# First norm computed with tokens on rows, c spread by a transfer, scale weights loaded ahead of shift weights; last norm applied while the output is turned back

## What is computed

```python
c_act = jax.nn.silu(c)                                  # c: 1024 values, one c per block
mod = (c_act @ w_ada[l] + b_ada[l]).reshape(B, N_SUB, 3, D_MODEL)   # shift, scale, gate of each step

def norm_mod(h, j):
    shift = mod[:, j, 0][:, None, :]
    scale = mod[:, j, 1][:, None, :]
    return _rms(h) * g_norm[l, j] * (1.0 + scale) + shift           # _rms: h / sqrt(mean(h*h) + eps)
...
x = x + gt2 * f                                         # the tenth step's residual
return rmsnorm(x, g_final)                              # the last norm, no shift
```

## Time and profile before

| | us |
|---|---|
| median of three timed runs | 1726.49 (1723.31 to 1727.04) |
| profiled execution | 1721.48 |
| its span, first to last instruction | 1719.6 |
| TensorE busy | 1644.6 |
| VectorE busy | 1324.5 |
| ScalarE busy | 905.6 |
| GpSimd busy | 96.8 |

### The profile page before, as it was taken

One profiled execution on the slowest core, in us unless ns is written; L12 is line 12 of the kernel. 1 busy time (PEld: TensorE's weight loads), 2 busy tenths in 40 slices (PEclk: granted clock), 3 DMA queues, 4 the chain that ended last, 5 costly groups with the idle time before them and its releaser, 6 DMA issues.

```text
span 1719.6 us, 31950 instructions
## 1 busy us (share of the span) xinstructions
PE 1644.6 (96%) x13282; PEld 1611.2 (94%) x13282; DVE 1324.5 (77%) x2089; ACT 905.6 (53%) x1554; POOL 96.8 (6%) x136
## 2 busy tenths in 40 slices
PE   2999999999999999999999999979999998899998
PEld 2999998999999999998999999968999998799998
DVE  7788889688888888888688888947888888385553
ACT  3444457664454544467554545645545456464443
POOL 6000000010000000100120001001000000010000
PEclk6999999999999999999999999989999999999999
DMA  8688675347877787854377878412787862145551
GB/s 327 244 326 318 270 282 196 123 175 310 320 289 278 284 324 295 316 205 168 113 273 299 323 286 308 144 52 99 289 324 304 308 249 103 70 146 198 176 192 50
DMA packets 56881, 402.19 MB, mean 234 GB/s; under 512 B 6574, under 2 KB 6706, under 8 KB 8992
## 3 DMA queue, kind: packets, MB, share of 16 engines
q1 hardware_dynamic: 55136, 394.97, 61.1%
q0 software_dynamic: 1600, 5.18, 1.0%
HBM read 399.06 MB, written 1.05 MB: 233 GB/s over the span
## 4 chain that ended last, share of the span: by engine, by line
PE 82%; DVE 12%; ACT 4%; issue 2%; DMA 0%; DVEq 0%; ACTq 0%
PE PS L494 81%; DVE WL L1559 3%; DVE ring L1584 2%; DVE SCR L1562 2%; DVE SCR L1559 1%; ACT SCR L1405 1%; ACT WH L1126 1%; DVE HL L1562 1%; DVE X L1562 1%; DVE SCR L1556 1%; ACT HH L1159 0%; DVE SMALL L1934 0%; DVE SQ L1562 0%; DVE SCR L1896 0%; DVE SMALL L1895 0%
## 5 line engine op out<-in xcount | busy, mean ns | idle before, releaser
L1559 DVE TENSOR_TENSOR WL<-ring,WH 128x1024 fp32r<-128x1024 f32 (+1 forms) x508 | 600.4, 1216 | 190.5 <-ACT WH L1126 190.2
L494 PE MATMUL PS<-HH,WH 128*128 128x256 f32 (+1 forms) x2640 | 651.9, 286 | 21.2 <-ACT WH L1126 18.5
L494 PE MATMUL PS<-HL,WH 128*128 128x256 f32 (+1 forms) x2640 | 640.5, 283 | 0.0
L1126 ACT ACTIVATE WH<-ring 128x1024 fp32r<-128x1024 f32 (+1 forms) x508 | 511.5, 1049 | 98.5 <-PE PS L494 53.5
L494 PEld LDWEIGHTS PS<-HH,WH 128*128 128x128 f32 x2640 | 497.7, 190 | 27.7 <-ACT WH L1126 19.2
L494 PEld LDWEIGHTS PS<-HL,WH 128*128 128x128 f32 x2640 | 495.6, 190 | 0.7
L494 PE MATMUL PS<-HH,WL 128*128 128x256 f32 (+1 forms) x2640 | 375.8, 280 | 2.0 <-DVE WL L1559 1.8
L494 PEld LDWEIGHTS PS<-HH,WL 128*128 128x128 f32 x2640 | 339.4, 189 | 3.3 <-DVE WL L1559 3.3
L1584 DVE CUSTOM_DVE_ANT_0 ring<-ring,CB,VC 128x1024 f32<-128x1024 f32 x240 | 317.5, 1347 | 0.0
L494 PE MATMUL PS<-AH,WL 128*128 128x256 f32 x1056 | 298.8, 283 | 0.0
L494 PE MATMUL PS<-AL,WH 128*128 128x256 f32 x1056 | 298.8, 283 | 0.0
(11 more groups left out here) (194 smaller groups left out, 1491.1 us busy)
## 6 DMA issues: line engine op xcount, KB each, us to landing
ring<-in_up SPq DMA_DIRECT2D x88, 1024.0 KB, 5.7
ring<-in_ada SPq DMA_DIRECT2D x72, 1024.0 KB, 6.9
ring<-in_ffn SPq DMA_DIRECT2D x66, 1024.0 KB, 4.8
ring<-in_mod SPq DMA_DIRECT2D x48, 1024.0 KB, 7.1
ring<-in_down SPq DMA_DIRECT2D x44, 1024.0 KB, 6.1
ring<-in_win SPq DMA_DIRECT2D x32, 1024.0 KB, 6.8
ring<-in_wout SPq DMA_DIRECT2D x16, 1024.0 KB, 4.8
ring<-in_winv SPq DMA_DIRECT2D x4, 1024.0 KB, 5.0
```

The lines of the kernel that those rows point to most:

```text
L494: return e.matmul(out, lhsT, rhs, start=start, stop=stop, skip_group_check=skip)
L1126: e.activation(half_of(i)[0], slot_of(("unit", u))[:, w * (i % 2):w * (i % 2) + w], ACT.Copy).then_inc(s_hi, 1)
L1559: return e.tensor_tensor(out, a, b, op)
```

## The change

- **Loads.** c of both blocks comes as two rows (`crow`); `spread_c` is now a transfer that writes one row to all 128 partitions of CB. That of the first block is issued third, that of the second behind load 13. x is issued behind the third ada panel. The scale panels 4 to 7 are loaded ahead of the shift panels 0 to 3.
- **Silu** is applied by ScalarE on CB, 128x1024, at once (first block at the start, second in the first feed-forward's step 16).
- **First norm.** ScalarE squares x_rows with a running sum per row (a token), makes the root per token and scales x_rows into xr_rows by it. TensorE turns both x_rows (for X) and xr_rows. ScalarE then makes SQ and HH of each chunk straight from PSUM, with gain and shift. VectorE does panels 4 to 7, `gains`, then one half of panels 0 to 3 and one chunk's remainder in turn. GpSimd's first additions are gone.
- **Last norm.** The gain is multiplied into X chunk by chunk (XG, ScalarE; the last on VectorE). TensorE turns XG back two chunks behind, between the matmuls of `out_proj`, and sums the squares per token with one-column matmuls. The root per token is applied by the copies from PSUM to OUT, half on ScalarE, half on VectorE.

```diff
-        loads = [("ada", i) for i in range(FIRST_ADA)] + [("unit", 0)]
+        loads = [("ada", (i + 4) % 8) for i in range(FIRST_ADA)] + [("unit", 0)]
...
@@ sync
-            e.dma_start(x_rows, A["x"].rearrange("(t p) d -> p t d", p=128)).then_inc(s_xload, 16)
+            def spread_c(v):
+                row = bass.AP(tensor=crow.tensor, offset=crow.offset + D * v, ap=[[0, 128], [1, D]])
+                e.dma_start(CB[:, v, :], row).then_inc(s_cload, 16)
+            spread_c(0)
...
+                if p == 2:
+                    e.dma_start(x_rows, A["x"].rearrange("(t p) d -> p t d", p=128)).then_inc(s_xload, 16)
+                if p == 13:
+                    spread_c(1)
...
-            for t in range(2):
-                for g in range(2):
-                    e.wait_ge(s_proj, 40 + 2 * t + g + 1)
+            for g in range(2):
+                for t, done in enumerate((s_fa, s_fd)):
+                    e.wait_ge(done, g + 1)
                     e.dma_start(A["out"][128 * t:128 * t + 128, 512 * g:512 * g + 512],
@@ gpsimd
-            square_sums(0)
             softplus()
@@ tensor
+            def turned_back(c):
+                e.wait_ge(*((s_xg, c + 1) if c < KD - 1 else (s_xgl, 1)))
+                for t in range(2):
+                    last = e.transpose(PS[:, (6 if c < 4 else 0) + t, 128 * (c % 4):128 * (c % 4) + 128], XG[:, c, 128 * t:128 * t + 128], ident)
+                if c % 4 == 3:
+                    last.then_inc(s_xt, 1)
+
+            def token_sums(c):
+                e.wait_ge(s_sq, 8 * NSUB - 8 + c + 1)
+                for t in range(2):
+                    last = mm(PS[:, 2, t:t + 1], SQ[:, c, 128 * t:128 * t + 128], one, start=c == 0 and t == 0, stop=c == KD - 1, skip=True)
+                if c == KD - 1:
+                    last.then_inc(s_fss, 1)
...
+                    if n == NSUB - 1 and k == kt - 1:
+                        if c >= 2:
+                            turned_back(c - 2)
+                        if c == 6:
+                            for b in range(5):
+                                token_sums(b)
+                if n == NSUB - 1:
+                    turned_back(6)
+                    token_sums(5)
+                    token_sums(6)
+                    token_sums(7)
+                    turned_back(7)
...
-            spread_c(0)
-            spread_c(1)
             e.wait_ge(s_xload, 16)
+            for rows, b in ((x_rows, 0), (xr_rows, 4)):
+                if b == 4:
+                    e.wait_ge(s_xr, 2)
+                for c in range(KD):
+                    for t in range(2):
+                        q = 256 * (c % 2) + 128 * t
+                        last = e.transpose(PS[:, b + c // 2, q:q + 128], rows[:, t, 128 * c:128 * c + 128], ident)
@@ scalar
+            e.wait_ge(s_cload, 16)
+            e.activation(CB[:, 0, :], CB[:, 0, :], ACT.Silu).then_inc(s_cb, 1)
             lnexp()
...
+            e.wait_ge(s_xload, 16)
+            for t in range(2):
+                step(e.activation(xr_rows[:, t, :], x_rows[:, t, :], ACT.Square, accum_out=rs0[:, t:t + 1]))
+            step(e.activation(rs0, rs0, ACT.Ln, bias=eps, scale=1.0 / D))
+            step(e.activation(rs0, rs0, ACT.Exp, scale=-0.5))
+            for t in range(2):
+                e.activation(xr_rows[:, t, :], x_rows[:, t, :], ACT.Copy, scale=rs0[:, t:t + 1]).then_inc(s_xr, 1)
+            for b in range(4):
+                e.wait_ge(s_xt, b + 1)
+                e.activation(X[:, 2 * b:2 * b + 2, :], pair(b), ACT.Copy).then_inc(s_x0, 1)
...
+            e.wait_ge(s_ab, 1)
+            for c in range(KD):
+                e.wait_ge(s_xt, 4 + c // 2 + 1)
+                if c % 2 == 0:
+                    e.wait_ge(s_shift, c // 2 + 1)
+                else:
+                    e.wait_ge(s_mod, 4 + c // 2 + 1)
+                xr, gain, shift = PS[:, 4 + c // 2, 256 * (c % 2):256 * (c % 2) + 256], AB[:, c:c + 1], MOD[:, c:c + 1]
+                e.activation(SQ[:, c, :], xr, ACT.Identity, bias=shift, scale=gain).then_inc(s_xn, 1)
+                e.activation(HH[:, c, 0:S], xr, ACT.Identity, bias=shift, scale=gain).then_inc(s_hh, 1)
+                if c == 5:
+                    hi_half(0)
+            hi_half(1)
...
+            e.wait_ge(s_fss, 1)
+            step(e.activation(rs1, PS[:, 2, 0:2], ACT.Ln, bias=eps, scale=1.0 / D))
+            step(e.activation(rs1, rs1, ACT.Exp, scale=-0.5))
+            e.activation(rs0, rs1, ACT.Copy).then_inc(s_frs, 1)
+            for g in range(2):
+                e.wait_ge(s_xt, 8 + g + 1)
+                e.activation(OUT[:, 0, 512 * g:512 * g + 512], PS[:, (6, 0)[g], :], ACT.Copy, scale=rs1[:, 0:1]).then_inc(s_fa, 1)
@@ vector
+            e.wait_ge(s_cb, 1)
+            ada_half(4, 0)
+            ada_half(4, 1)
...
+            for i in range(5, 8):
                 ada_half(i, 0)
                 ada_half(i, 1)
             gains(0)
+            for k in range(KD):
+                ada_half(k // 2, k % 2)
+                if k > 0:
+                    first_remainder(k - 1)
+            first_remainder(KD - 1)
             lo(0)
...
+            e.wait_ge(s_frs, 1)
+            for g in range(2):
+                e.wait_ge(s_xt, 8 + g + 1)
+                ts(OUT[:, 1, 512 * g:512 * g + 512], PS[:, (7, 1)[g], :], rs1[:, 1:2], None, ALU.mult, None).then_inc(s_fd, 1)
```

More of the change, by code:

```diff
@@ L494, in mm @@
                 return e.matmul(out, lhsT, rhs, start=start, stop=stop, skip_group_check=skip)
-            def spread_c(v):
-                for g in range(2):
-                    for k in range(4):
-                        j = KD * v + 4 * g + k
-                        last = mm(PS[:, 2 + 2 * v + g, 128 * k:128 * k + 128], ca_of(j).to_broadcast([128, 128]), ident)
-                    last.then_inc(s_cmm, 1)
             def cols(i, n, out, first):
@@ L1067, in _ @@
             e.wait_ge(s_const, 16)
-            e.wait_ge(s_c, 1)
-            spread_c(0)
-            spread_c(1)
             e.wait_ge(s_xload, 16)
-            for c in range(KD):
-                if c in (2, 4):
-                    e.wait_ge(s_cb, c // 2)
-                for t in range(2):
-                    last = e.transpose(PS[:, c % 6, 128 * t:128 * t + 128], x_rows[:, t, 128 * c:128 * c + 128], ident)
-                last.then_inc(s_xt, 1)
-                if c + 1 >= 6 and c + 1 < KD:
-                    e.wait_ge(s_x0, c - 4)
-            sum_squares(0)
+            for rows, b in ((x_rows, 0), (xr_rows, 4)):
[5 more added lines that the diff above has]
+                        last = e.transpose(PS[:, b + c // 2, q:q + 128], rows[:, t, 128 * c:128 * c + 128], ident)
+                    if c % 2:
+                        last.then_inc(s_xt, 1)
             for n, (kind, l, _) in enumerate(SUBS):
@@ L1093, in _ @@
                     bias_of_distance()
-            sum_squares(NSUB)
-            for t in range(2):
-                for g in range(2):
-                    for j in range(4):
-                        c = 4 * g + j
-                        e.wait_ge(s_xn, 80 + c + 1)
-                        last = e.transpose(PS[:, 2 * t + g, 128 * j:128 * j + 128], SQ[:, c, 128 * t:128 * t + 128], ident)
-                    last.then_inc(s_xt, 1)
         @block.scalar
@@ L1169, in renewed @@
                 square(n + 1, c)
+                if n + 1 == NSUB and c < KD - 1:
+                    e.activation(XG[:, c, :], X[:, c, :], ACT.Copy, scale=vec("gfinal", c)).then_inc(s_xg, 1)
             def down(n):
@@ L1202, in ffn @@
                         hi_half(2 * (UNIT0[n] + NF + 1))
+                    if n == 0 and f == 16:
+                        e.wait_ge(s_cload, 32)
+                        e.activation(CB[:, 1, :], CB[:, 1, :], ACT.Silu).then_inc(s_cb, 1)
                     if f >= 3:
@@ L1510, in mixer2 @@
                     renewed(n, c)
+            e.wait_ge(s_cload, 16)
+            e.activation(CB[:, 0, :], CB[:, 0, :], ACT.Silu).then_inc(s_cb, 1)
             lnexp()
-            e.wait_ge(s_vec, 16)
-            step(e.activation(cb, VC[:, VEC["c"]:VEC["c"] + 16], ACT.Exp, scale=-1.0))
-            e.wait_ge(s_const, 16)
-            for c in range(KD):
-                e.wait_ge(s_xt, c + 1)
-                e.activation(X[:, c, :], PS[:, c % 6, 0:256], ACT.Copy).then_inc(s_x0, 1)
-            for c in range(KD):
-                e.wait_ge(s_x0, c + 1)
-                square(0, c)
             e.wait_ge(s_lam, 1)
             e.activation(SM_[:, 136:144], SM_[:, 128:136], ACT.Exp, scale=-1.0).then_inc(s_lame, 1)
+            e.wait_ge(s_const, 16)
+            e.wait_ge(s_xload, 16)
[8 more added lines that the diff above has]
+                e.activation(X[:, 2 * b:2 * b + 2, :], pair(b), ACT.Copy).then_inc(s_x0, 1)
             for i in range(2):
                 e.activation(WFH[:, i, :], vec(f"wf{i}", 0, 32), ACT.Copy).then_inc(s_wfa, 1)
-            norm(0)
-            normalised(0)
-            hi(0)
```

(17 more changed lines are left out.)

79 lines of the change are left out of this document (36 added, 43 removed).

## The result

| | before | after |
|---|---|---|
| median of four runs each | 1725.5 us | 1713.34 us (1709.39 to 1714.51) |
| ratio, 95% interval | | 0.9923 (0.9908 to 0.9938) |
| profiled span | 1719.6 us | 1707.6 us |

The change is faster by 0.77% (13.3 us; by the interval 10.7 to 15.9). The forecast was 1719.3, 7.2 us faster, with a range from 1715.5. On another chip the same kernel gave 0.9909 (0.9894 to 0.9924).

A forecast was written before the change was run, and what follows sets the result against it. TensorE, busy 96% of the span, was taken as the bound except at the two ends. Head 5.7 us plus tail 1.5 (4.1 saved less 2.6 added) made 7.2, from 1726.49 to 1719.3 us; eight in ten within 1715.5 to 1723.8.

The forecast's parts named there:

- Head: when loads land: Start of the run: loads land 2.5 us apart, ada 4 at 10.5, x at 18.0, unit 0 at 33.0; queue never dry.
- rival 2: Loads or a slow VectorE stay the bound at the head, or the tail gives nothing: 1723.3 to 1723.8 us; chance 0.14.
- Head: CB: Start: the transfer repeating c's row lands at 7 (6.4 to 10.6), CB ready at 8.1 before ada 4, costing nothing.
- Rival 4: Slower: the one-row transfer to 128 partitions is slow; a landing at 24 gives 1730.7 us; chance 0.04.
- Head: VectorE: Start: ada panel halves at 1.20 us each, ada 4 from 10.5, ada 0 done at 25.5, then waiting for HH(0).
- Head: ScalarE: First norm: x reaches ScalarE at 18.0, scaled rows at 22.9, HH(0) at 26.3; VectorE has waited 0.8 us.
- the interleaved stretch: First norm from 26.3: halves and remainders alternate at 1.61 us; TensorE resumes at 38.7 instead of 44.49, 5.7 us earlier.
- Head: what comes behind: After TensorE's resumption: later unit loads, second CB transfer and its Silu cost nothing; clock rise one us off is 0.4 us.
- Tail: added to TensorE: Before the last residual: ten transposes, 1.4 us, and ten one-column matmuls, 1.2, add 2.6 us; bounds 2.4 to 4.0.
- Tail: after the last matmul: From the last residual's start to the end: 7.1 us instead of 11.2, saving 4.1.
- Sum: Whole kernel: head 5.7 plus tail 1.5 gives 7.2 us off the median 1726.49, so 1719.3 us.
- Rival 3: More than forecast: earlier queue (head 6.4), sooner clock rise (1.3), output at full rate (2.4): 10.1 us, 1716.4; chance 0.10.

The follow-up runs named there:

- head alone: Changed loads, scale and shift order and first norm, with the last norm of the kernel before and SBUF addresses as before: 1720.77 us, ratio 0.9970.
- tail alone: Kernel before with only the changed last norm put in, SBUF addresses as before: 1726.71 us, ratio 1.0006.
- both repairs: Changed kernel with GpSimd adding the last norm's squares for chunks 0 to 6 and x loaded one load sooner: 1709.68 us, ratio 0.9886.
- the same with 26 columns: Changed kernel with GpSimd adding the last norm's squares, x one load sooner and 26 unused columns ahead of the vectors: 1705.33 us, ratio 0.9861.

## Why the prediction was wrong, step by step

**Head: when loads land** — right to 0.4 us: ada 4 at 10.15 (10.5), x at 17.98 (18.0), ada 7 at 20.49 (20.5). The queue doesn't run dry, and the chain's first piece is the transfer of x, as rival 2 saw it, without its price.

**Head: CB** — right: at 7.1, forecast 7. The range's upper end, 8.9 from issue, wasn't needed; the transfer landed 5.4 from issue. The page "DMA: Bandwidth & Descriptors" (Rules for kernel authors) of the Trainium skill warns of broadcasts led by a short zero-stride dimension alone; with 128 copies leading, the trace agrees that nothing was lost. Rival 4 fell with it.

**Head: VectorE** — right: halves at 1.20 each. None ran at 1.6 any more, and GpSimd's additions beside them are gone.

**Head: ScalarE** and **the interleaved stretch** — HH(0) ends at 26.27 (26.3); a half and a remainder take 1.54 instead of 1.61; resumption at 38.43 (38.7), gain 6.1 for 5.7. The first weight half on ScalarE at 33.59 was as forecast, after unit 0.

**Head: what comes behind** — nothing lost, as said. The rise of the clock, priced at 0.4 for each us, came 2.3 us sooner behind the resumption, and made the head 7.2 in this profile. How much of that is the change's is not settled. In the eleven profiles with the changed head and x where the change puts it the clock rose 3.0 to 5.7 us behind the resumption, in the three with the old head 5.6 to 6.1, and their lead over the profile before, once the clock is up, is 5.6 to 7.2, 6.5 in the mean. The head alone has the least of these leads, 5.6, and was 5.2 us by its ratio. The forecast of 5.7 stands.

**Tail: added to TensorE** — the step that failed on the wrong side, mis-sized twice. First, ten one-column products were counted as ten instructions at 0.12. The trace took 20, at 0.107 each, 2.15 us for 1.2. The kernel before had shown it: sixteen one-column records belong to eight products in its code, and the 16 products of `spread_c` stand as x32 in the earlier trace rows. Each loads 128 columns of weights to stream one. The page "TensorE: Matmul & The Clock Gate" of the Trainium skill (LDWEIGHTS (loading the stationary operand)) puts such a load at its columns over 1.2, here 107 ns, and the trace agrees. Second, a stretch of such products can cost the clock behind them: 1.6 us in the profile above. With 1.1 for ten transposes (0.22 a pair for the forecast's 0.28) that is 4.9 where 2.6 was forecast and 4.0 was the upper bound. Without the loss of clock, 3.3 (tail alone).

**Tail: after the last matmul** — 7.5 for 7.1, a saving of 3.7 for 4.1. The first copies begin 2.3 (ScalarE) and 2.4 (VectorE) behind the residual's start (forecast 2.1, as sum 7's two products are four instructions), the first output transfer is issued at 3.0 (2.8), and the four landed 2.5 us from issue (median), so the faster of the two rates that the forecast weighed was the right one. So the tail was worth 0 to -1 us instead of 1.5: measured 1.0006 by itself.

**Sum.** Head 5.2 to 5.7 and tail 0 make 5 us with the places as before: 0.9972 measured, 1721.7 for 1726.49, within the range. The other two kernels with AH where it was gave 0.9957 and 0.9942, still within it. What took the result out of it is one term that the sum didn't have: the removed columns moved the scratch area by 64 bytes, worth 7 us in the down projections, and 1 more in the profile where part of the last one ran at the third level. That they moved it the faster way is luck, as nobody chose it. The step at fault is the first paragraph's "nothing in the middle that only lightens another engine can move the time": it looked at what TensorE waits for and not at how fast its own instructions run. Rival 3 named the right side, but for three causes of which none held in full.

**Could it have been read from the profile before?** The 0.120 us from start to start in the down projections was there to see, and the diff takes 16 columns out of VC. No row of before shows another value in these stages, so the price wasn't there; that all addresses behind VC shift, an unknown with two sides on every matmul, was, and it had no place in the range.

## What to carry to other kernels

When a change adds or drops a small tile or some columns, all tiles behind it move, and the matmuls of whole stages may run 2% faster or slower for it: here those of six down projections. Before a part is credited or blamed, run it once with spare columns that put the large tiles back; then try the places on purpose, for it is the cheapest gain to be had here: 7 us for a change of 64 bytes, against 5 for rewriting both norms. And count levels stage by stage before two profiles are compared: one slow up projection more is 1.6 us that neither kernel has earned. Of work put between the matmuls of the bounding engine, count the instructions as the profile counts them, and keep one-column products out of a full stream: the sums on GpSimd were free.

## What the runs showed of the hardware

- Matmuls of 128x256 whose weights and whose streamed operand begin at the same place within 128 bytes start every 0.1200 us, with places 64 bytes apart every 0.1178, and in some stages of some runs every 0.1133. In the up projections, whose streamed chunks lie at many places, it is 0.1180 or 0.1197 with the weights at 0 and 0.1192 with them at 64. A level changes only at a gap in the row of matmuls. The page "TensorE: Matmul & The Clock Gate" of the Trainium skill (Step-by-step: what each phase is for) says that weights and streamed operand have ports of their own and that loading the one steals nothing from the other. Here the time of a matmul depends on where the one lies against the other, so the two aren't independent; the measurement decides.
- Twenty one-column instructions (ten products) in a row in a stream at full clock are followed by a halved clock in seven of eleven profiles (the last chunk took 11.55 to 11.86 us) and not in four (10.23 to 10.37). The clock can fall elsewhere too: the kernel with both repairs at 330 us, and the same with 26 columns, columns as above:

```profile
330.50:336.00 5.50, 5.50 (x37) 5.50 (x36) 2.79 (x9) 2.65 (x7) 0.00 (x0) 0.69 0.27 110
```

```profile
330.00:336.00 6.00, 6.00 (x54) 6.00 (x53) 4.70 (x11) 3.39 (x8) 0.00 (x0) 1.00 0.27 113
```

  The same instructions behind the same idle of 1.79 us on TensorE lose 1.5 us (1.89 against 0.34 us between the two kernels) in the one run and nothing in the other. The two profiles of the changed kernel differ by 3.4 us (1707.6 and 1711.0) for another reason: 3.1 of it arise in two up projections that ran at 0.1197 in the second.
- A transfer that repeats one row of 4 KB on 128 partitions landed 5.4 us from its issue, behind 0.4 MB of others.
